# Last output block and final norm in two token halves of 128, the other output blocks of layer 1 with both activation parts in one 512-column product

## The chip, the cores and the metric

The kernel runs on one core of one Trainium2 chip. The metric is device time in microseconds of one execution. Three runs of the kernel before gave a median of 1247.78 us (1247.63 to 1248.28).

## What is computed

Two layers of a mixer on 256 latent tokens and 256 context tokens of width 2048, then a norm of the latent tokens. Each layer normalises and modulates its input, projects it by `w_in`, runs three branches (convolution, linear recurrence, windowed attention), gates each, and ends in one output projection. Cut to what the change touches:

```python
    x = x + gate * (jnp.concatenate([y_conv, y_lru, y_attn], axis=-1) @ w_out)
    ...
def rmsnorm(x, g):
    xf = x.astype(jnp.float32)
    y = xf * lax.rsqrt(jnp.mean(xf * xf, axis=-1, keepdims=True) + EPS)
    return (y * g.astype(jnp.float32)).astype(x.dtype)
    ...
    return rmsnorm(x, final_g)
```

In the last layer only the 256 latent tokens (`LAT`) go through the output projection.

## The kernel before, in words

Everything is held transposed: the 128 partitions are features, the free axis is tokens, and a tensor of 2048 features is 16 tiles (`DT`) of 128 x `TOK` (512: first 256 latent, then 256 context). A product with a 2048 x 128 weight block is 16 k tiles, accumulated in one bank of PSUM. To keep accuracy in the reduced format float32r, weights and activations are split in a high part (rounded) and a low part (the rest), and each k tile takes three products: high weights x high activations (line 826), high weights x low activations (L827), low weights x high activations (L828). Every product loads its own 128 x 128 weights.

Each layer has 56 blocks of 128 output features in the order of `BLOCKS`; the last 16 (`B_OUT` to `NB - 1`) are the output projection. The weight stream is one list (`stream()`): SyncE loads a block of 1 MB into one of three raw slots; ScalarE rounds half a block into `w_hi` (`hi`, L1050), VectorE subtracts to get `w_lo` (`lo`, L1410), into one of four slots each. Both run two blocks ahead of TensorE, in the program order of the loops over `gb`. Every engine has its own program; they meet only in semaphores (`C.up` raises, `C.at` names a value to wait for).

Of layer 1's output projection (its activations lie in the token columns 256 to 511 of `h_hi` and `h_lo`, `y_parts`):

- TensorE, `mm_half` (L803): half a block of eight k tiles, twice a block; waits for `lo` and for the bank (two banks in turn, `released`). It raises `mm`.
- VectorE, `evac` (L1581): once a block is done, Y = PSUM x gate + Y for the 256 latent tokens (L1614). In VectorE's order it stands behind both `lo` halves of the block two ahead. Then `rms_add` (L1467) adds a squared tile to the running sum.
- ScalarE, `square` (L1066, the operation is L1079) squares the new tile of Y and `scaled` (L1083) writes the tile times `final_g` to the other half of Y's columns.
- After the last block: TensorE sums over partitions with a product by ones (`rms_mm`, L714: the sum of 15 squares at L723, then the last square at L725), ScalarE takes the root (`rms_std`, L1101), VectorE the reciprocal (`rstd`, L1549) and five multiplications over 2, 4, 4, 4 and 2 tiles (`FINAL`, L1890), and SyncE stores each of the five pieces when it is ready (L618).

Layer 0's last two blocks are already done in token halves of 256 (`evac_lat`, `rms_mm_half` with L731 and L733), with their waits hidden by other products.

Of the kernel before, what the change touches and what calls it, by code (L numbers as in the profile page):

```python
# [24 lines left out]
P = 128  # L25
# [42 lines left out]
SPAN = (1, 1, 1, 1, 1, 1, 1, 1)  # L68
GROUPS = len(SPAN)
XPART = 2  # L70
FINAL = (2, 4, 4, 4, 2)
HALF = DT // 2 * P
BRIDGE = [14, 4, 6, 8]
SPLIT_FROM = NB - 2
# [177 lines left out]
def program(nc, io, known):  # L252
    ctx = ExitStack()
    with ctx:
# [12 lines left out]
        NRAW = 3  # L267
        GLU_SLOT, Q_SLOTS, KV_SLOT, BD_SLOT = NRAW, (NRAW + 1, NRAW + 2), NRAW + 3, NRAW + 4
        ADA0_SLOTS, CHUNK_SLOTS = (*range(NRAW), GLU_SLOT, KV_SLOT, BD_SLOT), Q_SLOTS
        hh = sb("h_hi", [P, DT, TOK], F32R)  # L270
        hl = sb("h_lo", [P, DT, TOK], F32R)
        Y = sb("Y", [P, DT, TOK])
        raw = sb("raw", [P, NRAW, DT * P])
        wh = sb("w_hi", [P, 4, DT // 2 * P], F32R)
# [166 lines left out]
        def done_before(l, b):  # L441

            last = PLAN.get(b - 1, []) if l == 0 else PLAN[NB] if b == OPEN[l] else []
            return [a[:2] for a in last if a[2] == DT - 1]

        def width(l, b):
            return TOK if l == 0 or BLOCKS[l][b][0] in BOTH else LAT

# [14 lines left out]
        def in_halves(gb):  # L463
            return SPLIT_FROM <= gb < NB

        def final_parts():
            return [(sum(FINAL[:i]), n) for i, n in enumerate(FINAL)]

        def squares(l):

            return (2, 3) if l else (0, 1, 2, 3)
# [45 lines left out]
        def _(sp):  # L517
# [49 lines left out]
            for i, item in enumerate(STREAM):  # L567
# [45 lines left out]
                    residual(item[1] - B_OUT - 2)  # L613
                elif item[0] == "open" and item[1] < 2:
                    residual(DT - 2 + item[1])
            for m, n in final_parts():
                sp.wait_ge(*C.at("final", m))
                sp.dma_start(io["out"][:, m:m + n, :], Y[:, m:m + n, 0:LAT]).then_inc(*C.up("stored", by=16))  # L618
            sp.wait_ge(*C.ago("stored"))


# [23 lines left out]
        def _(pe):  # L645
# [67 lines left out]

            def rms_mm(l):  # L714

                n = TOK if l < LAYERS else LAT
                if l == 0:
                    pe.wait_ge(*C.at("rms_add", l, DT - 1))
                    mm(psS[:, 0, 0:n], ones, T[:, 4, 0:n], start=True, stop=True).then_inc(*C.up("rms_mm", l))
                    return  # L720
                assert l == LAYERS
                pe.wait_ge(*C.at("rms_add", l, DT - 2))
                mm(psS[:, 0, 0:n], ones, T[:, 4, 0:n], start=True, stop=False)  # L723
                pe.wait_ge(*C.at("rms_sq", l, DT - 1))
                mm(psS[:, 0, 0:n], ones, T[:, squares(l)[(DT - 1) % 2], 0:n], start=False, stop=True).then_inc(*C.up("rms_mm", l))  # L725

            def rms_mm_half(s):

# [74 lines left out]
            def mm_half(gb, j, s=None):  # L803
                l, b = divmod(gb, NB)
                n = width(l, b)
                ps = bank(gb)
                u = unit(l, b, j)
                pe.wait_ge(*C.at("lo", u))
                if j == 0 and b == PW_AT + 1:
                    pe.wait_ge(*C.at("pw_out", l, CT - 2))  # L810
                elif j == 0 and b >= OPEN[l] and s != 1:
                    pe.wait_ge(*released(gb - 2 if b - 2 >= OPEN[l] else l * NB + b % 2))
                slot = u % 4
                t = y_parts(l) if b >= B_OUT else slice(0, n)
                cols = slice(0, n)
                if s is not None:
                    t = cols = tokens(s)
                if s == 1 and j == 0:
                    pe.wait_ge(*C.at("evac_lat", gb))
                for i in range(DT // 2):  # L820
                    at = j * DT // 2 + i
                    k = k_tile(b, at)
                    if b == B_OUT:
                        pe.wait_ge(*C.at("y_lo", l, k))
                    hi, lo = wh[:, slot, i * P:(i + 1) * P], wl[:, slot, i * P:(i + 1) * P]
                    mm(ps[:, cols], hi, hh[:, k, t], start=(at == 0), stop=False)  # L826
# [150 lines left out]
            for gb in range(GLOB):  # L977
# [14 lines left out]
                if in_halves(gb):  # L992
                    mm_half(gb, 0, 0)
                    mm_half(gb, 1, 0)
                    if b == NB - 1:
                        mm_half(gb - 1, 0, 1)
                        rms_mm_half(0)
                        mm_half(gb - 1, 1, 1)
                        mm_half(gb, 0, 1)
                        mm_half(gb, 1, 1)  # L1000
                    continue
                mm_half(gb, 0)

                for a in done_before(l, b):
# [29 lines left out]
                elif l == 0:  # L1034
                    for a in PLAN.get(b, []):
                        ada_mm(*a)
            rms_mm(LAYERS)


        @block.scalar  # L1040
        def _(act):
# [41 lines left out]
            def scaled(m):  # L1083
                fn(Y[:, m, LAT:TOK], Y[:, m, 0:LAT], ACT.Copy, scale=at["final_g"][:, m:m + 1]).then_inc(*C.up("scaled", m))

            def square_half(m, s):
# [9 lines left out]
                fn(tbuf[:, w], psS[:, 2 + s, w], ACT.Sqrt, scale=1.0 / D, bias=eps[:, 0:1]).then_inc(*C.up("rms_std", 1, s))  # L1096

            def rms_std(l):
                n = TOK if l < LAYERS else LAT
                act.wait_ge(*C.at("rms_mm", l))  # L1100
                fn(tbuf[:, 0:n], psS[:, 0, 0:n], ACT.Sqrt, scale=1.0 / D, bias=eps[:, 0:1]).then_inc(*C.up("rms_std", l))  # L1101

# [282 lines left out]
                    y_hi(l, b)  # L1385
            act.wait_ge(*C.at("derived"))
            fn(tiny[:, 0, 0:1], eps[:, 0:1], ACT.Sqrt).then_inc(*C.up("root_ahead"))
            square(LAYERS, DT - 1)
            rms_std(LAYERS)
            scaled(DT - 1)  # L1390


        @block.vector
        def _(dve):
# [149 lines left out]
                h_list([(QT, 1)] + [(k, i) for k in range(QT + 1, 2 * QT) for i in range(2)])  # L1544

            def rstd(l):
                n = TOK if l < LAYERS else LAT
                dve.wait_ge(*C.at("rms_std", l))
                V.reciprocal(tbuf[:, 0:n], tbuf[:, 0:n]).then_inc(*C.up("rstd", l))  # L1549
                dve.wait_ge(*C.ago("rstd"))  # L1550

            def h_chunk(c):

# [27 lines left out]
            def evac(gb):  # L1581
# [200 lines left out]
            for gb in range(GLOB):  # L1782
# [48 lines left out]
                    lo(unit(0, gb + 2, 1))  # L1831
                if gb == GLOB - 1:
                    rms_add(LAYERS, DT - 2)
                if in_halves(gb):
                    evac_half(gb, 0)
                elif l or b != B_OUT - 1:
                    evac(gb)
# [56 lines left out]

# [69 lines left out]
```

## Time and profile before

| what | before |
|---|---|
| median of three runs | 1247.78 us |
| the profiled execution | 1247.64 us |
| its span, first to last record | 1245.7 us |
| TensorE busy | 1203.5 us, 97% |
| VectorE busy | 827.3 us, 66% |
| ScalarE busy | 555.5 us, 45% |
| mean granted TensorE clock | 0.995 of full |
| DMA moved | 236.34 MB, 190 GB/s |

How to read it: times in all rows are from the span's start. A busy record of TensorE (PE) has a modelled end and overlaps the next one, so the spacing of starts, not the length of a record, tells what a product costs; PEld are the weight loads, which run beside the products. DVE is VectorE, ACT ScalarE, SPq the queue of SyncE that issues DMAs.

### The profile page before, as it was taken

Reading aid. Unit: us, or ns where it says so; the run is one execution under the profiler, and the core shown is the slowest. Engines: PE = TensorE matmul, PEld = TensorE weight load, DVE = VectorE, ACT = ScalarE, POOL = GpSimd, SP = SyncE. Lnnn points to the kernel's source line nnn. Section 1 sums busy time; section 2 is a strip of 40 time slices with the busy share of each in tenths; the row PEclk is TensorE's granted clock in tenths of the full one; section 3 lists DMA queues with packets and bytes.
Section 4 is the critical chain, followed back from the end, with each engine's and each line's share of the span. In section 5 each row is a group of like instructions: output and inputs, shape, how many; then the busy total and the mean of one; then the engine's idle time right before and its main releaser. Section 6 shows DMA issues by size and latency. Waiting matters only on the chain.

```text
span 1245.7 us, 16857 instructions
## 1 busy us (share of the span) xinstructions
PE 1203.5 (97%) x6790; PEld 971.9 (78%) x6790; DVE 827.3 (66%) x1268; ACT 555.5 (45%) x873; POOL 10.2 (1%) x13
## 2 busy tenths in 40 slices
PE   2899999999999999999999999999999999999996
PEld 1556777667778777886888887988978988899995
DVE  5444546767666677663787877695899977647554
ACT  5222446652224433464342222354865445475542
POOL 0000100000000000000000001000000000000000
PEclk9999999999999999999999999999999999999998
DMA  9999856556753354211549776343332634325542
GB/s 334 350 349 348 251 208 240 203 207 248 270 218 127 140 187 185 75 68 68 177 158 344 259 286 229 109 145 134 138 106 77 223 133 149 132 102 199 177 170 68
DMA packets 80893, 236.34 MB, mean 190 GB/s; under 512 B 9392, under 2 KB 54192, under 8 KB 59440
## 3 DMA queue, kind: packets, MB, share of 16 engines
q1 hardware_dynamic: 80816, 235.27, 53.5%
q8 instruction: 53, 0.87, 0.3%
q14 instruction: 24, 0.20, 0.1%
HBM read 230.54 MB, written 2.10 MB: 187 GB/s over the span
## 4 chain that ended last, share of the span: by engine, by line
PE 84%; DVE 5%; SPq 4%; DMA 4%; ACT 2%; issue 1%; DVEq 0%; ACTq 0%
PE psum_block L826 21%; PE psum_block L828 21%; PE psum_block L827 21%; SPq L602 3%; PE psum_ada L656 3%; DMA raw<-in_w_ada 2%; PE psum_scores L908 1%; PE psum_scores L895 1%; DVE w_lo L1410 1%; PE psum_scores L928 1%; DVE Y L1691 1%; PE psum_ada L703 1%; DMA glu<-in_w_ada 1%; DMA bd<-in_w_ada 1%; PE psum_misc L955 1%; PE psum_scores L858 1%
## 5 line engine op out<-in xcount | busy, mean ns | idle before, releaser
L826 PE MATMUL psum_block<-h_hi,w_hi 128*128 128x256 f32 (+1 forms) x1648 | 562.4, 341 | 0.6 <-DVE h_lo L1402 0.3
L828 PE MATMUL psum_block<-h_hi,w_lo 128*128 128x256 f32 (+1 forms) x1648 | 553.3, 336 | 0.0
L827 PE MATMUL psum_block<-h_lo,w_hi 128*128 128x256 f32 (+1 forms) x1648 | 553.2, 336 | 0.0
L1410 DVE TENSOR_TENSOR w_lo<-raw,w_hi 128x1024 fp32r<-128x1024 f32 x210 | 254.7, 1223 | 287.7 <-ACT w_hi L1050 287.4
L1050 ACT ACTIVATE w_hi<-raw 128x1024 fp32r<-128x1024 f32 x210 | 220.2, 1057 | 419.5 <-PE psum_block L828 380.0
L826 PEld LDWEIGHTS psum_block<-h_hi,w_hi 128*128 128x128 f32 x1648 | 312.7, 190 | 53.4 <-issue 17.6
L827 PEld LDWEIGHTS psum_block<-h_lo,w_hi 128*128 128x128 f32 x1648 | 312.9, 190 | 33.6 <-issue 2.6
L828 PEld LDWEIGHTS psum_block<-h_hi,w_lo 128*128 128x128 f32 x1648 | 312.7, 190 | 32.4
L1691 DVE SCALAR_TENSOR_TENSOR Y<-glu,small,Y 128x512 f32<-128x512 f32 (+1 forms) x240 | 130.4, 612 | 0.0
L1217 ACT ACTIVATE T<-psum_scores,stats 128x512 f32<-128x512 f32 (+1 forms) x48 | 28.9, 615 | 46.5 <-DVE stats L1739 46.5
L1104 ACT ACTIVATE h_hi<-T,ada 128x256 fp32r<-128x256 f32 x64 | 28.5, 501 | 41.6 <-DVE T L1486 41.6
L1410 DVE TENSOR_TENSOR w_lo<-qreg,w_hi 128x1024 fp32r<-128x1024 f32 (+1 forms) x16 | 17.5, 1092 | 33.4 <-ACT w_hi L1050 32.3
L656 PE MATMUL psum_ada<-raw,cstat 128*32 128x512 f32 x320 | 38.5, 598 | 1.1 <-DVE ada L1475 1.1
L1444 DVE SCALAR_TENSOR_TENSOR kv<-raw,cstat,kv 128x2048 f32<-128x2048 f32 x15 | 35.2, 2344 | 1.1 <-DMA raw<-in_w_ada 1.0
L1223 ACT ACTIVATE T<-T,stats 128x512 f32<-128x512 f32 (+1 forms) x48 | 27.4, 640 | 13.6 <-DVE stats L1749 13.6
L1648 DVE SCALAR_TENSOR_TENSOR Y<-qreg,small,Y 128x512 f32<-128x512 f32 x48 | 32.5, 746 | 0.0
L1050 ACT ACTIVATE w_hi<-qreg 128x1024 fp32r<-128x1024 f32 (+1 forms) x16 | 15.1, 945 | 33.8 <-DMA qreg<-in_w_blocks 33.8
L1079 ACT ACTIVATE T<-Y 128x512 f32<-128x512 f32 (+1 forms) x46 | 24.4, 544 | 10.8 <-DVE Y L1614 8.6
L1492 DVE SCALAR_TENSOR_TENSOR h_lo<-T,ada,h_hi 128x256 fp32r<-128x256 f32 x64 | 27.8, 480 | 1.3 <-ACT h_hi L1104 1.3
L1486 DVE SCALAR_TENSOR_TENSOR T<-Y,A,tbuf 128x256 f32<-128x256 f32 x64 | 27.6, 481 | 0.6
L1456 DVE SCALAR_TENSOR_TENSOR qreg<-glu,cstat,qreg 128x2048 f32<-128x2048 f32 x12 | 27.6, 2345 | 0.0
L1467 DVE TENSOR_TENSOR T<-T 128x512 f32<-128x512 f32 (+1 forms) x42 | 25.1, 598 | 2.8 <-ACT T L1079 1.3
(222 smaller groups left out, 1215.0 us busy)
## 6 DMA issues: line engine op xcount, KB each, us to landing
raw<-in_w_blocks SPq DMA_DIRECT2D x105, 1024.0 KB, 4.8
raw<-in_w_ada SPq DMA_DIRECT2D x75, 1024.0 KB, 7.1
glu<-in_w_ada SPq DMA_DIRECT2D x11, 1024.0 KB, 8.1
qreg<-in_w_blocks SPq DMA_DIRECT2D x8, 896.0 KB, 11.6
kv<-in_w_ada SPq DMA_DIRECT2D x5, 1024.0 KB, 12.0
bd<-in_w_ada SPq DMA_DIRECT2D x5, 1024.0 KB, 11.9
Y<-in_xT SPq DMA_DIRECT2D x8, 512.0 KB, 8.0
T<-in_xT SPq DMA_DIRECT2D x16, 256.0 KB, 5.8
```

The costliest lines, as they stand in the source:

```text
L602: sp.dma_start(dst, src).then_inc(C.sem(f"raw{SLOT[i]}"), 16)
L656: last = mm(psA[32 * j:32 * j + 32, :], cstat[:, c_at(k):c_at(k) + 32], w[:, j * TOK:(j + 1) * TOK], start=(k == 0), stop=(k == DT - 1), t ...
L826: mm(ps[:, cols], hi, hh[:, k, t], start=(at == 0), stop=False)
L827: mm(ps[:, cols], hi, hl[:, k, t], start=False, stop=False)
L828: last = mm(ps[:, cols], lo, hh[:, k, t], start=False, stop=(at == DT - 1))
L1050: fn(wh[:, u % 4, 0:cols.stop - cols.start], raw_of(item)[:, cols], ACT.Copy).then_inc(*C.up("hi", u))
L1104: fn(hh[:, k, tokens(i)], T[:, k % 2, tokens(i)], ACT.Identity, bias=ada[:, l, i, SHIFT * DT + k:SHIFT * DT + k + 1]).then_inc(*C.up("h_hi ...
L1217: fn(T[:, g, k0:TOK], psS[:, g, k0:TOK], ACT.Exp, scale=SCALE, bias=st[:, 1, g:g + 1], accum_out=st[:, 2, g:g + 1]).then_inc(*C.up("att_ex ...
L1410: V.tensor_tensor(wl[:, u % 4, 0:n], raw_of(item)[:, cols], wh[:, u % 4, 0:n].bitcast(F32), ALU.subtract).then_inc(*C.up("lo", u))
L1444: stt(acc, w, cstat[:, c_at(k):c_at(k) + 1], acc, ALU.mult, ALU.add).then_inc(*C.up("gate_acc", k))
L1648: stt(out, x, lcw[:, c, k:k + 1], out, ALU.mult, ALU.add).then_inc(*C.up("taps", l, t, d))
L1691: stt(out, x, dwh[:, c:c + 1], out, ALU.mult, ALU.add).then_inc(*C.up("conv", l, t, k))
```

## The change

It does two things, both in layer 1's output projection.

One: the high and low activations become two halves of one tensor, `parts`. In the output blocks of layer 1 except the last (`apart`), the products of lines 826 and 827 become one with 512 columns: its first 256 columns of PSUM hold high x high, to which low weights x high activations are added, its other 256 high weights x low activations. `evac` adds the second half of the bank to Y first (a new operation, with a wait behind it), then the first half as before.

Two: the last block runs in two halves of 128 tokens (`LAST`): products of the first token half for both halves of k, then those of the second; evacuation, square, sum, root, reciprocal, multiplications and store are done for each token half. The multiplications go over 8 and 8 tiles for the first half, 6, 6 and 4 for the second.

```diff
-FINAL = (2, 4, 4, 4, 2)
+FINAL = ((8, 8), (6, 6, 4))
+LAST = LAT // len(FINAL)
...
-        hh = sb("h_hi", [P, DT, TOK], F32R)
-        hl = sb("h_lo", [P, DT, TOK], F32R)
+        parts = sb("h_parts", [P, 2, DT, TOK], F32R)
+        hh, hl = parts[:, 0, :, :], parts[:, 1, :, :]
...
+        def apart(l, b):
+
+            return l == 1 and B_OUT <= b < NB - 1
...
-            for m, n in final_parts():
-                sp.wait_ge(*C.at("final", m))
-                sp.dma_start(io["out"][:, m:m + n, :], Y[:, m:m + n, 0:LAT]).then_inc(*C.up("stored", by=16))
+            for s in range(len(FINAL)):
+                for m, n in final_parts(s):
+                    sp.wait_ge(*C.at("final", s, m))
+                    sp.dma_start(io["out"][:, m:m + n, last_tokens(s)], Y[:, m:m + n, last_tokens(s)]
+                                 ).then_inc(*C.up("stored", by=16))
...
+            def last_rms_mm(s):
+
+                w = last_tokens(s)
+                pe.wait_ge(*C.at("rms_add", LAYERS, DT - 2))
+                mm(psS[:, s, w], ones, T[:, 4, w], start=True, stop=False)
+                pe.wait_ge(*C.at("rms_sq", LAYERS, DT - 1, s))
+                mm(psS[:, s, w], ones, T[:, squares(LAYERS)[(DT - 1) % 2], w], start=False, stop=True
+                   ).then_inc(*C.up("rms_mm", LAYERS, s))
+
+            def last_block_half(j, s):
+
+                gb = GLOB - 1
+                u = unit(1, NB - 1, j)
+                if s == 0:
+                    pe.wait_ge(*C.at("lo", u))
+                    if j == 0:
+                        pe.wait_ge(*released(gb - 2))
+                elif j == 0:
+                    pe.wait_ge(*C.at("evac_lat", gb))
+                w = last_tokens(s)
+                t = slice(LAT + w.start, LAT + w.stop)
+                ps = bank(gb)[:, w]
+                for i in range(DT // 2):
+                    at = j * DT // 2 + i
+                    k = k_tile(NB - 1, at)
+                    hi, lo = wh[:, u % 4, i * P:(i + 1) * P], wl[:, u % 4, i * P:(i + 1) * P]
+                    mm(ps, hi, hh[:, k, t], start=(at == 0), stop=False)
+                    mm(ps, hi, hl[:, k, t], start=False, stop=False)
+                    last = mm(ps, lo, hh[:, k, t], start=False, stop=(at == DT - 1))
+                if j:
+                    last.then_inc(*C.up("mm_last", s))
...
+                    if apart(l, b):
+                        mm(segs(ps), hi, parts[:, :, k, t], start=(at == 0), stop=(at == DT - 1))
+                        last = mm(ps[:, cols], lo, hh[:, k, t], start=False, stop=(at == DT - 1), skip_group_check=True)
+                        continue
...
+                if gb == GLOB - 1:
+                    last_block_half(0, 0)
+                    last_block_half(1, 0)
+                    last_block_half(0, 1)
+                    last_rms_mm(0)
+                    last_block_half(1, 1)
+                    last_rms_mm(1)
+                    continue
...
-            square(LAYERS, DT - 1)
-            rms_std(LAYERS)
-            scaled(DT - 1)
+            last_square(0)
+            last_std(0)
+            last_scaled(0)
+            last_square(1)
+            last_std(1)
+            last_scaled(1)
...
+                    if apart(l, b):
+                        stt(Y[:, i, 0:LAT], bank(gb)[:, LAT:TOK], ada[:, l, 0, GATE * DT + i:GATE * DT + i + 1],
+                            Y[:, i, 0:LAT], ALU.mult, ALU.add).then_inc(*C.up("low_part", gb))
+                        dve.wait_ge(*C.ago("low_part"))
...
-            rstd(LAYERS)
-            dve.wait_ge(*C.ago("evac_dve"))
-            for m, n in final_parts():
-                for k in range(m, m + n):
-                    dve.wait_ge(*C.at("scaled", k))
-                V.tensor_tensor(Y[:, m:m + n, 0:LAT], Y[:, m:m + n, LAT:TOK],
-                                tbuf[:, 0:LAT].unsqueeze(1).to_broadcast([P, n, LAT]), ALU.mult).then_inc(*C.up("final", m))
+            last_evac(0)
+            last_rstd(0)
+            last_evac(1)
+            finals(0)
+            last_rstd(1)
+            finals(1)
```

`last_square`, `last_std`, `last_scaled`, `last_evac`, `last_rstd` and `finals` are the operations of before on the columns of one token half; `last_evac(0)` raises `evac_lat`.

## Rows read from the trace of the kernel before

**Rows 1.** The page: busy time by engine (sections 1 and 4).
```profile
PE 1203.5 (97%) x6790; PEld 971.9 (78%) x6790; DVE 827.3 (66%) x1268; ACT 555.5 (45%) x873; POOL 10.2 (1%) x13
...
PE 84%; DVE 5%; SPq 4%; DMA 4%; ACT 2%; issue 1%; DVEq 0%; ACTq 0%
```

**Rows 2.** Timeline (start, length, engine, line, operation): first product of two blocks.
```profile
1140.20 0.28 PE L826 MATMUL psum_block<-h_hi,w_hi 128*128 128x256 f32 x1
...
1226.61 0.28 PE L826 MATMUL psum_block<-h_hi,w_hi 128*128 128x256 f32 x1
```

**Rows 3.** Stretch of the last block: busy by engine, granted clock, DMA share, GB/s.
```profile
1226.61:1232.37 5.76, 5.76 (x51) 5.76 (x50) 1.24 (x3) 2.31 (x4) 0.00 (x0) 1.00 0.00 0
```

**Rows 4.** Timeline of the tail.
```profile
1232.37 0.59 PE L723 MATMUL psum_scores<-T,small 128*128 128x256 f32 x2
1232.57 0.48 DVE L1614 SCALAR_TENSOR_TENSOR Y<-psum_block,ada,Y 128x256 f32<-128x256 f32 x1 [4.37 <-PE psum_block L828]
1233.09 0.42 ACT L1079 ACTIVATE T<-Y 128x256 f32<-128x256 f32 x1 [3.42 <-DVE Y L1614]
...
1234.29 0.47 ACT L1101 ACTIVATE tbuf<-psum_scores,eps 128x256 f32<-128x256 f32 x1 [0.79 <-PE psum_scores L725]
...
1234.80 1.75 DVE L1549 RECIPROCAL tbuf<-tbuf 128x256 f32<-128x256 f32 x1 [1.75 <-ACT tbuf L1101]
1236.59 4.70 DVE L1890 TENSOR_TENSOR Y<-Y,tbuf 128x512 f32<-128x512 f32 x5
1237.31 4.67 SPq L618 DMA_DIRECT2D out<-Y  x5
```

**Rows 5.** DMA of 1236 to 1246 us, GB/s in forty slices of 0.25 us.
```profile
GB/s 0 0 0 0 0 0 0 0 25 319 348 324 33 152 356 344 340 291 381 340 344 340 348 295 381 332 336 348 311 377 340 340 356 340 303 45 0 0 0 0
```

**Rows 6.** Timeline of TensorE, layer 0: 512-column products, the first and the twelfth.
```profile
599.66 0.39 PE L826 MATMUL psum_block<-h_hi,w_hi 128*128 128x512 f32 x1
...
602.15 0.39 PE L828 MATMUL psum_block<-h_hi,w_lo 128*128 128x512 f32 x1
```

**Rows 7.** Groups by line: count, busy us, mean ns, idle before.
```profile
L858 PE MATMUL psum_scores<-Y,bd 128*128 128x512 f32 x32 | 14.4, 592 | 0.0
L928 PE MATMUL psum_scores<-T,kv 128*128 128x512 f32 x32 | 14.4, 592 | 0.0
```

**Rows 8.** Timeline of VectorE: low activation parts, and a block's evacuation.
```profile
1143.50 1.42 DVE L1402 TENSOR_TENSOR h_lo<-Y,h_hi 128x256 fp32r<-128x256 f32 x4
...
1223.34 0.48 DVE L1614 SCALAR_TENSOR_TENSOR Y<-psum_block,ada,Y 128x256 f32<-128x256 f32 x1
```

**Rows 9.** Timeline of products and weight loads around one 128-column product, layer 0.
```profile
369.10 0.22 PE L886 MATMUL psum_scores<-rounded 128*128 128x128 f32 x1
...
369.44 0.40 PE L882 MATMUL psum_scores<-kv_r,T_r 128*128 128x512 f32 x1
...
369.10 0.19 PEld L881 LDWEIGHTS psum_scores<-bd_r,T_r 128*128 128x128 f32 x1
369.21 0.19 PEld L882 LDWEIGHTS psum_scores<-kv_r,T_r 128*128 128x128 f32 x1
```

**Rows 10.** Timeline: eight transposes of 128 columns.
```profile
602.38 1.03 PE L908 MATMUL psum_scores<-rounded,T 128*128 128x128 f32 x8
```

**Rows 11.** Groups by line: one operation at other sizes.
```profile
L1549 DVE RECIPROCAL tbuf<-tbuf 128x512 f32<-128x512 f32 x1 | 3.4, 3353 | 4.3 <-ACT tbuf L1101 4.3
...
L1890 DVE TENSOR_TENSOR Y<-Y,tbuf 128x1024 f32<-128x1024 f32 x3 | 3.5, 1219 | 0.0
...
L1890 DVE TENSOR_TENSOR Y<-Y,tbuf 128x512 f32<-128x512 f32 x2 | 1.4, 688 | 0.0
```

**Rows 12.** Timeline of TensorE: layer 0's norm product inside the stream.
```profile
796.38 0.59 PE L731 MATMUL psum_scores<-T,small 128*128 128x256 f32 x2
...
797.36 0.28 PE L827 MATMUL psum_block<-h_lo,w_hi 128*128 128x256 f32 x1
```

**Rows 13.** Stretch of one microsecond, all engines, clock, DMA share, GB/s.
```profile
656.00:657.00 1.00, 1.00 (x6) 0.81 (x6) 0.89 (x1) 0.35 (x1) 0.00 (x0) 1.00 1.33 245
```

More of the change, by code:

```diff
@@ L464, in in_halves, with final_parts, last_tokens @@
             return SPLIT_FROM <= gb < NB
-        def final_parts():
-            return [(sum(FINAL[:i]), n) for i, n in enumerate(FINAL)]
+        def final_parts(s):
+            return [(sum(FINAL[s][:i]), n) for i, n in enumerate(FINAL[s])]
+        def last_tokens(s):
+            return slice(s * LAST, (s + 1) * LAST)
         def squares(l):
@@ L714, in rms_mm @@
             def rms_mm(l):
[L716 to L725, printed above, removed]
+                assert l == 0
+                pe.wait_ge(*C.at("rms_add", l, DT - 1))
+                mm(psS[:, 0, :], ones, T[:, 4, :], start=True, stop=True).then_inc(*C.up("rms_mm", l))
+            def last_rms_mm(s):
[26 more added lines that the diff above has]
+                    last.then_inc(*C.up("mm_last", s))
             def rms_mm_half(s):
@@ L1036, in _ @@
                         ada_mm(*a)
-            rms_mm(LAYERS)
         @block.scalar
@@ L1084, in scaled, with last_square, last_std, last_scaled @@
                 fn(Y[:, m, LAT:TOK], Y[:, m, 0:LAT], ACT.Copy, scale=at["final_g"][:, m:m + 1]).then_inc(*C.up("scaled", m))
+            def last_square(s):
+                w = last_tokens(s)
+                act.wait_ge(*(C.at("evac_dve", GLOB - 1) if s else C.at("evac_lat", GLOB - 1)))
+                act.wait_ge(*C.at("rms_add", LAYERS, DT - 3))
+                fn(T[:, squares(LAYERS)[(DT - 1) % 2], w], Y[:, DT - 1, w], ACT.Square).then_inc(*C.up("rms_sq", LAYERS, DT - 1, s))
+            def last_std(s):
+                w = last_tokens(s)
+                act.wait_ge(*C.at("rms_mm", LAYERS, s))
+                fn(tbuf[:, w], psS[:, s, w], ACT.Sqrt, scale=1.0 / D, bias=eps[:, 0:1]).then_inc(*C.up("rms_std", LAYERS, s))
+            def last_scaled(s):
+                w = last_tokens(s)
+                fn(Y[:, DT - 1, LAT + w.start:LAT + w.stop], Y[:, DT - 1, w], ACT.Copy, scale=at["final_g"][:, DT - 1:DT]
+                   ).then_inc(*C.up("last_scaled", s))
             def square_half(m, s):
@@ L1098, in rms_std @@
             def rms_std(l):
-                n = TOK if l < LAYERS else LAT
+                n = TOK
                 act.wait_ge(*C.at("rms_mm", l))
@@ L1546, in rstd, with last_evac, last_rstd, finals @@
             def rstd(l):
-                n = TOK if l < LAYERS else LAT
                 dve.wait_ge(*C.at("rms_std", l))
-                V.reciprocal(tbuf[:, 0:n], tbuf[:, 0:n]).then_inc(*C.up("rstd", l))
+                V.reciprocal(tbuf[:, :], tbuf[:, :]).then_inc(*C.up("rstd", l))
                 dve.wait_ge(*C.ago("rstd"))
+            def last_evac(s):
+                w = last_tokens(s)
+                dve.wait_ge(*C.at("mm_last", s))
+                stt(Y[:, DT - 1, w], bank(GLOB - 1)[:, w], ada[:, 1, 0, GATE * DT + DT - 1:GATE * DT + DT], Y[:, DT - 1, w],
+                    ALU.mult, ALU.add).then_inc(*(C.up("evac_dve", GLOB - 1) if s else C.up("evac_lat", GLOB - 1)))
+            def last_rstd(s):
+                w = last_tokens(s)
+                dve.wait_ge(*C.at("rms_std", LAYERS, s))
+                V.reciprocal(tbuf[:, w], tbuf[:, w]).then_inc(*C.up("rstd", LAYERS, s))
+                dve.wait_ge(*C.ago("rstd"))
+            def finals(s):
+                w = last_tokens(s)
+                for m, n in final_parts(s):
+                    for k in range(m, min(m + n, DT - 1)):
+                        dve.wait_ge(*C.at("scaled", k))
+                    if m + n == DT:
+                        dve.wait_ge(*C.at("last_scaled", s))
+                    V.tensor_tensor(Y[:, m:m + n, w], Y[:, m:m + n, LAT + w.start:LAT + w.stop],
+                                    tbuf[:, w].unsqueeze(1).to_broadcast([P, n, LAST]), ALU.mult).then_inc(*C.up("final", s, m))
             def h_chunk(c):
@@ L1833, in _ @@
                     rms_add(LAYERS, DT - 2)
+                    continue
                 if in_halves(gb):
```

## The prediction

> **What bounds the kernel now.** I read the page first: TensorE is busy 97% of the span and holds 84% of the chain that ended last [rows 1]. Then the timeline of TensorE in the last hundred microseconds. From the first output block of layer 1 to the last one (1140.20 to 1226.61) it runs 15 blocks of 48 products of 256 columns without a gap: 86.41 us / 720 = 0.120 us a product, 5.76 us a block [rows 2]. The granted clock of the last block is full speed, 2.4 GHz, and no DMA is under way in it [rows 3]. So each nanosecond taken off a product there reaches the end. After the last product (1232.37) comes a serial tail of 13.3 us [rows 4]: evacuation, square, sum over partitions, root, reciprocal, five multiplications, and the store. The DMA view of the last ten microseconds shows what ends last [rows 5]: 2.10 MB leave at about 340 GB/s, nearly without a pause from 1239.5 to 1244.8, though the last piece is computed at 1241.29. The end of the kernel is the store's rate, counted from when its first pieces are ready.
>
> **Part 1, both activation parts in one product (15 blocks).** Per k tile, two products of 256 columns become one of 512. In layer 0 eleven spacings of 512-column products take 602.15 - 599.66 = 2.49 us, 0.226 each [rows 6]. Two of 256 cost 0.240. The gain is 0.0133 us per k tile (0.2267 and 0.120 lie on a line of 0.0133 + 0.000417 per column), x 16 x 15 = 3.2 us. The product now reads two segments far apart. The nearest rows are layer 1's gate products, which read two segments, against the attention products, which read 512 columns in one run: 592 ns both [rows 7]. Those segments lie one tile apart instead of sixteen; I take no cost, and 3.2 us (all of the gain gone) as the other end. A gain beyond 0.0133 is excluded, since the columns streamed are the same.
>
> The evacuation of each of these blocks becomes two dependent operations: one more of 0.48 us on VectorE. The evacuation of the fourteenth block now starts at 1223.34 [rows 8], 2.5 us after that block's last product (1226.61 - 5.76 = 1220.85), because `lo` of a later block stands before it; with the second one it ends some 3.5 us after. The bank is wanted again 5.55 us after that last product, so it costs nothing; it would with 2 us more on VectorE. In the first output block TensorE comes to its last four k tiles at 1140.20 + 12 x 0.347 = 1144.36 and then every 0.35 us; their low parts are made from 1143.50 on, 0.35 us each [rows 8]: ready about half a microsecond ahead. No cost, but little slack. The last block's weights are split two blocks ahead; that stays hidden. The last block so starts at 1226.61 - 3.2 = 1223.4.
>
> **Part 2, the last block in two token halves.** Its 48 products of 256 columns become 96 of 128. If the columns alone counted, the line above would give 0.067 us each. But each product loads its own 128 x 128 weights. One 128-column product of this number format stands between 512-column ones in the score groups of layer 0 [rows 9]: from its start (369.10) to that of the second product behind it (369.44) are 0.34 us, of which the 512-column one is 0.227, so it cost 0.11; and the two weight loads after it begin 0.11 apart (369.10, 369.21), the second only when the first is in the array. Eight 128-column transposes in a row take 1.03 us with the last one's drain, at most 0.129 each [rows 10]. I take 0.108 as the spacing. The Trainium skill, TensorE: Matmul & The Clock Gate, section LDWEIGHTS (loading the stationary operand), gives columns / 1.2 ns, 107 ns for 128 columns; by that rule, the trace agrees, and it speaks against splitting this block. So 96 x 0.108 = 10.37 us instead of 5.76.
>
> On top: the second token half waits for `evac_lat`, the evacuation of the first, with nothing of TensorE's own queued between; all later products stand behind that wait. Before, VectorE starts 0.20 us after the last product's slot and takes 0.48 [rows 4]; for 128 columns I put 0.17 + 0.345 (the 1.04 ns per element by which 1024 and 512 elements differ, 1219 and 688 ns [rows 11]), 0.04 for the signal and about 0.15 to load and restart: 0.7 us idle, 0.5 to 0.9. And the first half's norm product now stands between products: in layer 0 the same four passes at 256 columns delay the stream by 797.24 - 796.38 = 0.86 us [rows 12] (797.24 is 0.12 before the next start); at 128 columns four loads of 0.108 bound it below, 0.43, and I take 0.45.
>
> TensorE after: 1223.4 + 5.18 (first half) + 0.7 + 2.59 + 0.45 + 2.59 = 1234.9, against 1232.37: 2.6 us later in spite of part 1.
>
> **The tail.** Evacuation of the second half starts at 1235.1 and ends at 1235.45. By then the first half's root and reciprocal (3353 ns for 512 elements, 1755 for 256 [rows 4, 11], so 0.96 for 128) are done, about 1234.0: in the shadow of the last 24 products. The multiplications of the first half are queued on VectorE ahead of the second reciprocal: two of 1024 elements, 1.22 each, to 1237.8. Square, sum and root of the second half end about 1236.7 in their shadow. Then reciprocal 0.96 and multiplications 0.95 + 0.95 + 0.69, with handoffs: 1241.3. Before, the multiplications ended at 1236.59 + 4.70 = 1241.29. So VectorE's end does not move: half-size reciprocal and earlier multiplications give back what TensorE lost.
>
> **The store.** The first piece (512 KB) is ready at 1235.45 + 1.22 = 1236.7. Before, the first was issued at 1237.31 and bytes moved from about 1238.1: 0.8 us. Now they move from 1237.5, and each next piece is ready before the one ahead has left, so 2.10 MB run through without a pause. But pieces of a row are 512 bytes, not 1 KB. The nearest rows: 1 KB pieces move at about 340 GB/s [rows 5], and in a microsecond in which the gate weights come in, in pieces of 64 numbers (256 bytes), the engines move 245 [rows 13]. I take the middle, 290: 7.24 us, so the last byte at 1244.7, against 1244.8. At 340 it would be 1.1 us earlier, at 245 1.3 later. The Trainium skill, DMA: Bandwidth & Descriptors, Specifications, asks for at least 512 B for line rate; by it alone the sum would be 1.1 us lower. No row here has 512-byte pieces.
>
> **Sum.** -0.1 us on the profiled execution (1247.64 with a span of 1245.7, 1.9 around it): 1247.5. That run lay 0.14 under the median of the three, 1247.78, so 1247.7. Bounds of this case: below, -1.1 (store), -0.2 (shorter restart) and -0.5 (the small operations at 128 columns start from fewer fixed costs than the line says): 1245.9. Above, a spacing of 0.120 as now, where the 0.0133 comes on top of the load (+1.15), +1.3 (store), +0.2: 1250.3.
>
> **Rivals.** (a) *The columns set the pace of the halves*: 0.067 instead of 0.108, if consecutive loads overlap further in a long run than after one product. TensorE ends 96 x 0.041 = 3.9 us earlier, and all after it shifts: 1243.7, faster. The records of the loads, 0.19 long at spacings of 0.12, overlap already and speak for it; the two loads 0.11 apart [rows 9] and the transposes against. The skill's TensorE page, section Back-to-back issue gap, has 81 ns for sustained 128-column products; worked out, 96 x 0.027 = 2.6 us earlier, 1245.1. Chance 7%.
> (b) *The merged product gains nothing*: a two-segment read or the switch between a 512- and a 256-column product eats the 0.0133 us. It decides from the price where the pair costs 0.240 instead of 0.227. Then the last block starts 3.2 us later, nothing hides it, and the run takes 1250.9: slower. Only [rows 7] speak against, for another number format. 7%.
> (c) *The clock falls in the last block.* At 0.108 a product the array streams half of the time, and it idles 0.7 us once; the last block before has the full clock [rows 3] with the array nearly always streaming. If the level falls to 1.2 GHz over the second token half, its 48 products cost up to 5.2 us more: about 1252.9. 5%.
> (d) *The split does not do what it says*: the store's start is all that counts, and it moves only 0.6 us earlier; that is inside my forecast.
>
> **How the numbers follow.** Forecast case 80%, (a) 7, (b) 7, (c) 5, other 1. About 0.2% (2.5 us) is what a measurement of this kernel can tell from no change: 1245.3 to 1250.3. Faster: (a), 7%, plus 2% of the forecast's lower end. Slower: (b), (c), and 2% of its upper end, 14%. Same: 77%. The forecast's own bounds, 1245.9 to 1250.3, hold close to 8 in 10, and I keep them.
>
> **What would show it.** Products of the 14 undisturbed blocks: a start every 0.227 + 0.120 us, 5.55 us a block. Last block: starts 0.107 to 0.113 apart, one gap of about 0.7 us in the middle; its last product near 1235. VectorE's last multiplication near 1241.3. The store flowing from 1237.5 without a pause to about 1244.7, at 290 GB/s. Starts 0.067 apart would show (a), a block of 5.76 us (b), a granted clock under 1 before 1235 (c). A store at 340 GB/s would take a microsecond off and leave the verdict.

## The result

| | before | after |
|---|---|---|
| median | 1247.86 us (16 runs) | 1250.03 us (16 runs) |
| ratio, 95% interval | | 1.0018 [1.0012, 1.0024] |
| span of the profiled execution | 1245.7 us | 1248.0 us |
| TensorE instructions | 6790 | 6602 |

The change makes the kernel 0.18% slower. That is less than the 0.2% that I called the limit of what can be told, but the interval does not contain 1: my forecast was 0.1 us less, in effect no movement, and the 2.2 us more are real. The profile after, against the rows of before.

The page, against [rows 1]: 188 fewer products, yet TensorE is busy 4.6 us more.
```profile
PE 1208.1 (97%) x6602; PEld 965.0 (77%) x6602; DVE 834.8 (67%) x1285; ACT 557.2 (45%) x876; POOL 10.2 (1%) x13
```
The timeline of TensorE, against [rows 2] and [rows 6]: start, length, engine and line. L862 is the merged product, L863 the low weights' product.
```profile
1140.27 0.40 PE L862 MATMUL psum_block<-h_parts,w_hi 128*128 128x512 f32 x1
1140.50 0.28 PE L863 MATMUL psum_block<-h_parts,w_lo 128*128 128x256 f32 x1
1140.62 0.40 PE L862 MATMUL psum_block<-h_parts,w_hi 128*128 128x512 f32 x1
1140.86 0.28 PE L863 MATMUL psum_block<-h_parts,w_lo 128*128 128x256 f32 x1
1140.98 0.40 PE L862 MATMUL psum_block<-h_parts,w_hi 128*128 128x512 f32 x1
...
1225.07 0.22 PE L756 MATMUL psum_block<-h_parts,w_hi 128*128 128x128 f32 x1
```
240 pairs, each a merged product and a low weights' product, take 1225.07 - 1140.27 = 84.80 us, 0.3533 each: not the 0.360 of before, and not the 0.347 that I had summed. The next product starts 0.23 or 0.24 us after a 512-column one and 0.11 or 0.12 us after a 256-column one. Half of the gain of part 1 is missing, 1.6 us.

The last block, against [rows 2, 3]:
```profile
1225.24 0.27 PE L758 MATMUL psum_block<-h_parts,w_lo 128*128 128x128 f32 x1
...
1230.27 0.27 PE L758 MATMUL psum_block<-h_parts,w_lo 128*128 128x128 f32 x1
1230.98 0.33 PE L756 MATMUL psum_block<-h_parts,w_hi 128*128 128x128 f32 x1 [0.44 <-DVE Y L1622]
1231.15 0.27 PE L757 MATMUL psum_block<-h_parts,w_hi 128*128 128x128 f32 x1
...
1233.72 0.43 PE L734 MATMUL psum_scores<-T,small 128*128 128x128 f32 x2
...
1234.28 0.27 PE L757 MATMUL psum_block<-h_parts,w_hi 128*128 128x128 f32 x1
```
The stretch of this block (busy by engine, granted clock, DMA share, GB/s):
```profile
1225.07:1236.85 11.78, 11.34 (x103) 11.20 (x101) 3.03 (x6) 3.28 (x7) 0.00 (x0) 1.00 0.00 1
```
45 spacings of the first half take 1230.27 - 1225.24 = 5.03 us, 0.112 each. In the middle stands the wait for the evacuation of the first half: from 1230.27 to 1231.15 are 0.88 us where two spacings would be 0.22, so 0.66 idle. The norm product costs 1234.28 - 0.11 - 1233.72 = 0.45.

The tail, against [rows 4]:
```profile
1236.85 0.43 PE L734 MATMUL psum_scores<-T,small 128*128 128x128 f32 x2
1237.11 0.35 DVE L1622 SCALAR_TENSOR_TENSOR Y<-psum_block,ada,Y 128x128 f32<-128x128 f32 x1 [1.35 <-PE psum_block L758]
...
1237.51 2.36 DVE L1640 TENSOR_TENSOR Y<-Y,tbuf 128x1024 f32<-128x1024 f32 x2
...
1238.77 5.56 SPq L627 DMA_DIRECT2D out<-Y  x5
1239.79 0.95 DVE L1629 RECIPROCAL tbuf<-tbuf 128x128 f32<-128x128 f32 x1
1240.77 2.43 DVE L1640 TENSOR_TENSOR Y<-Y,tbuf 128x768 f32<-128x768 f32 x3
```
TensorE is done at 1236.85 instead of 1232.37. The first piece of the store is issued at 1238.77, 1.5 us later than before, and what comes out of it is the store's flow, 1238 to 1248 us in slices of 0.25 us, against [rows 5]:
```profile
GB/s 0 0 0 0 0 0 29 291 291 293 291 225 274 317 279 293 287 293 254 276 307 289 289 285 225 328 287 281 295 254 303 295 289 289 287 287 109 0 0 0
```
Bytes move from 1239.6 to 1247.1, without a pause, at about 290 GB/s between dips and 285 with them; before it was 340, dips included.

### The profile page after: what moved, and what is told of

Read it like the earlier page. It is cut to its first block, busy times and chain, and to the rows that moved or that the text cites. A ratio compares the mean times of both kernels' runs of the same rounds, so it can differ in the third digit from the quotient of the medians.

```text
span 1248.0 us, 16510 instructions
## 1 busy us (share of the span) xinstructions
PE 1208.1 (97%) x6602; PEld 965.0 (77%) x6602; DVE 834.8 (67%) x1285; ACT 557.2 (45%) x876; POOL 10.2 (1%) x13
## 4 chain that ended last, share of the span: by engine, by line
PE 82%; DVE 6%; SPq 4%; DMA 4%; ACT 3%; issue 1%; DVEq 0%; ACTq 0%
PE psum_block L865 18%; PE psum_block L866 18%; PE psum_block L867 18%; PE psum_block L862 5%; SPq L610 3%; PE psum_ada L666 3%; PE psum_block L863 2%; DMA raw<-in_w_ada 2%; DVE w_lo L1477 2%; DVE Y L1786 2%; PE psum_scores L934 1%; PE psum_scores L947 1%; DMA glu<-in_w_ada 1%; PE psum_ada L713 1%; DMA bd<-in_w_ada 1%; PE psum_misc L994 1%
## 5 line engine op out<-in xcount | busy, mean ns | idle before, releaser
L865 PE MATMUL psum_block<-h_parts,w_hi 128*128 128x512 f32 (+1 forms) x1392 | 490.0, 352 | 0.7 <-DVE h_parts L1469 0.3
L866 PE MATMUL psum_block<-h_parts,w_hi 128*128 128x512 f32 (+1 forms) x1392 | 480.8, 345 | 0.0
L867 PE MATMUL psum_block<-h_parts,w_lo 128*128 128x512 f32 (+1 forms) x1392 | 480.8, 345 | 0.0
L865 PEld LDWEIGHTS psum_block<-h_parts,w_hi 128*128 128x128 f32 x1392 | 263.6, 189 | 53.6 <-issue 17.6
L866 PEld LDWEIGHTS psum_block<-h_parts,w_hi 128*128 128x128 f32 x1392 | 263.8, 189 | 33.4 <-issue 2.6
L867 PEld LDWEIGHTS psum_block<-h_parts,w_lo 128*128 128x128 f32 x1392 | 263.6, 189 | 32.4
L862 PE MATMUL psum_block<-h_parts,w_hi 128*128 128x512 f32 x240 | 84.8, 399 | 0.0
L863 PE MATMUL psum_block<-h_parts,w_lo 128*128 128x256 f32 x240 | 67.4, 281 | 0.0
L862 PEld LDWEIGHTS psum_block<-h_parts,w_hi 128*128 128x128 f32 x240 | 45.1, 188 | 11.3
L1168 ACT ACTIVATE h_parts<-T,ada 128x256 fp32r<-128x256 f32 x64 | 28.6, 503 | 42.6 <-DVE T L1553 42.6
L863 PEld LDWEIGHTS psum_block<-h_parts,w_lo 128*128 128x128 f32 x240 | 45.3, 189 | 0.0
L1559 DVE SCALAR_TENSOR_TENSOR h_parts<-T,ada,h_parts 128x256 fp32r<-128x256 f32 x64 | 27.8, 481 | 1.3 <-ACT h_parts L1168 1.3
```

The lines of the kernel that those rows point to most:

```text
L862: mm(segs(ps), hi, parts[:, :, k, t], start=(at == 0), stop=(at == DT - 1))
```

## Experiments

Profiled executions differ by up to 1.5 us in when the output blocks of layer 1 begin (1139.6 to 1141.0 us), also between kernels that are the same up to there. Where I compare profiles I therefore count from the first product of these blocks to the end of the span: 105.5 us before, 107.7 after.

**The two parts apart.** The kernel before with part 1 alone, so without the change to the last block (shown is TensorE's edit; the joined tensor and the second evacuation operation go with it):
```diff
+                    if apart(l, b):
+                        mm(segs(ps), hi, parts[:, :, k, t], start=(at == 0), stop=(at == DT - 1))
+                        last = mm(ps[:, cols], lo, hh[:, k, t], start=False, stop=(at == DT - 1), skip_group_check=True)
+                        continue
```


> Part 1 of the change alone: the merged products in the first 15 output blocks of layer 1, last block, norm and store as before. By the trace of the changed kernel the pair of products takes 0.353 us instead of 0.360, so 15 blocks save 1.6 us, all of which must reach the end: 1246.2 us, ratio 0.9987. If the changed kernel's slower pair comes from something that the merged product does to the stream only together with the split last block, the gain would be the 3.2 us that I had summed: 1244.6. If merging also disturbs the tail (a later evacuation ahead of the last block), nothing is gained: 1247.8.

Measured: 1245.71 us, ratio 0.9986 [0.9977, 0.9994]. From the first output block to the end 103.9 us, 1.6 less than before. The other way round, the last block in halves and no merged product:
```diff
-            return l == 1 and B_OUT <= b < NB - 1
+            return False
```


> Part 2 alone: last block, norm and store in two token halves, all other blocks as before. If the parts add, this is the changed kernel plus 1.6 us: 1251.6 us, ratio 1.0030. By the prediction's own terms for this part (products 0.108 apart, store at 290 GB/s) it would be 1250.7. If the split were innocent and the merge the cause of the loss, it would lie at or under 1247.8.

Measured: 1251.56 us, ratio 1.0033 [1.0021, 1.0046]; 109.3 us from the first output block, 3.8 more than before. The parts add up: -1.6 + 3.8 = 2.2 in the profiles, and in the medians, each against the kernel before in the same round, -1.8 + 4.0 = 2.2. Part 1 is a gain, and part 2 costs more than twice as much.

**Why the pair takes 0.353 us.** Three kernels, each the merge alone with one thing changed. Each ran once, so I read its profile and not its time. The merged product reads one run of 512 columns (the output blocks of layer 1 then compute something else):
```diff
-                        mm(segs(ps), hi, parts[:, :, k, t], start=(at == 0), stop=(at == DT - 1))
+                        mm(ps, hi, hh[:, k, :], start=(at == 0), stop=(at == DT - 1))
```


> As the merge alone, but the merged product reads 512 columns in one run of the high activations (latent and context columns) instead of two segments 16 tiles apart; this changes what is computed in the output blocks of layer 1, and only the spacing of the products counts. If the two-segment read costs the missing 6.7 ns of a pair, pairs are 0.347 us apart. If it is the change between a 512- and a 256-column product, or the 256-column product adding to columns just written, they stay at 0.353.

Measured: still 0.353, in the same pattern of 0.24 and 0.12 (1180.83 - 1179.77 = 1.06 us for three pairs). The timeline of TensorE in this kernel:
```profile
1179.77 0.40 PE L831 MATMUL psum_block<-h_parts,w_hi 128*128 128x512 f32 x1
1180.01 0.28 PE L832 MATMUL psum_block<-h_parts,w_lo 128*128 128x256 f32 x1
1180.13 0.40 PE L831 MATMUL psum_block<-h_parts,w_hi 128*128 128x512 f32 x1
1180.37 0.28 PE L832 MATMUL psum_block<-h_parts,w_lo 128*128 128x256 f32 x1
1180.48 0.40 PE L831 MATMUL psum_block<-h_parts,w_hi 128*128 128x512 f32 x1
1180.71 0.28 PE L832 MATMUL psum_block<-h_parts,w_lo 128*128 128x256 f32 x1
1180.83 0.40 PE L831 MATMUL psum_block<-h_parts,w_hi 128*128 128x512 f32 x1
```
So the two segments are not the cause. The work of other engines beside the stream is hardly the cause either: by the start times of the merge alone in nanoseconds, its 479 spacings repeat 233, 117, 241, 120, 236, 113 to within a nanosecond through all 15 blocks, whatever VectorE and ScalarE do at the time. The low product added to the other half of the bank:
```diff
-                        last = mm(ps[:, cols], lo, hh[:, k, t], start=False, stop=(at == DT - 1), skip_group_check=True)
+                        last = mm(ps[:, LAT:TOK], lo, hh[:, k, t], start=False, stop=(at == DT - 1), skip_group_check=True)
```


> As the merge alone, but the low weights' product is added to the second half of the bank instead of the first; the result is the same, since both halves are added up. If the loss comes from adding to columns that were written a given time before, the spacing of 0.353 us a pair changes (in the first half 512 columns lie between a column's two writes, in the second only 256). If it comes from the read or from the change of sizes, it stays at 0.353.

Measured: 0.353 again (103.9 us from the first output block, as in the merge alone). Which columns of PSUM are added to does not matter. Two merged products, then the two low ones:
```diff
-                        last = mm(ps[:, cols], lo, hh[:, k, t], start=False, stop=(at == DT - 1), skip_group_check=True)
+                        if i % 2:
+                            for o in (1, 0):
+                                last = mm(ps[:, cols], wl[:, slot, (i - o) * P:(i - o + 1) * P], hh[:, k_tile(b, at - o), t], start=False,
+                                          stop=(at == DT - 1 and o == 0), skip_group_check=True)
```


> As the merge alone, but two merged products are followed by the two low products, so that the size changes half as often. If each change of size costs, the mean of a pair falls from 0.353 to 0.350 us. If each two-segment read costs, it stays at 0.353. If a weight load is what is late behind a 256-column product, two of these in a row make it worse, above 0.353.

Measured: 0.348 a k tile, and 102.6 us from the first output block, 1.2 less than the merge alone. Its timeline, where consecutive products of one line are one row:
```profile
1180.24 0.62 PE L831 MATMUL psum_block<-h_parts,w_hi 128*128 128x512 f32 x2
1180.70 0.40 PE L834 MATMUL psum_block<-h_parts,w_lo 128*128 128x256 f32 x2
1180.93 0.63 PE L831 MATMUL psum_block<-h_parts,w_hi 128*128 128x512 f32 x2
```
Four products take 1180.93 - 1180.24 = 0.69 us (0.697 over the whole stream), where two alternating pairs take 0.707. The order of the sizes makes the difference. Is it each change of size? The same with groups of eight:
```diff
-                        if i % 2:
-                            for o in (1, 0):
+                        if i % 8 == 7:
+                            for o in range(7, -1, -1):
```


> As the merge alone, but eight merged products are followed by the eight low products of the half block. The mean of a k tile was 0.3533 us with alternating sizes and 0.3483 in groups of two. If the change of size is all that is lost, groups of eight come to the 0.2267 + 0.1200 = 0.3467 us that I had predicted, or a little above: 15 blocks then save 3.2 us against the kernel before: 1244.4 us, ratio 0.9974. If instead two short products behind two long ones are served faster than in a long run (in groups of two they stood 0.114 apart), eight are no better than two: 0.348 or more.

Measured: 1245.31 us, ratio 0.9983 [0.9974, 0.9992]. The timeline shows two things.
```profile
1140.44 2.00 PE L831 MATMUL psum_block<-h_parts,w_hi 128*128 128x512 f32 x8
1142.28 1.11 PE L834 MATMUL psum_block<-h_parts,w_lo 128*128 128x256 f32 x8
1143.23 2.47 PE L831 MATMUL psum_block<-h_parts,w_hi 128*128 128x512 f32 x8
1145.55 1.11 PE L834 MATMUL psum_block<-h_parts,w_lo 128*128 128x256 f32 x8
1146.49 2.00 PE L831 MATMUL psum_block<-h_parts,w_hi 128*128 128x512 f32 x8
...
1180.01 2.00 PE L831 MATMUL psum_block<-h_parts,w_hi 128*128 128x512 f32 x8
1181.85 1.11 PE L834 MATMUL psum_block<-h_parts,w_lo 128*128 128x256 f32 x8
1182.80 2.00 PE L831 MATMUL psum_block<-h_parts,w_hi 128*128 128x512 f32 x8
```
In the middle of the stream eight k tiles take 2.79 us, 0.349 each: above the 0.347 of my sum, and no better than groups of two. The eight long products take 1.84 (0.230 each, where the 0.2267 of [rows 6] would give 1.81), the short ones 0.95 (0.119). And in the first output block the second group takes 2.32 instead of 1.84: its last four tiles stand 0.5 to 0.9 us earlier than in the alternating order, and now TensorE waits for their low parts. VectorE makes these four parts in this row:
```profile
1143.73 1.43 DVE L1413 TENSOR_TENSOR h_parts<-Y,h_parts 128x256 fp32r<-128x256 f32 x4
```
That is about 0.35 us each, and the last four long products of the group are 0.33 to 0.34 apart. The slack that I had called little was half a microsecond, and this order used it up, 0.5 us in all.

So the loss stands behind a change of size, but not as a fixed price per change: that would have made eights the best. By the start times in nanoseconds, the spacings after the eight long products of a group are 233, 236, 228, 233, 231, 226, 227, 227, and those after the short ones 113, 119 and then 120: the first five long products behind the change are dearer by 28 ns together, the first short ones cheaper by 8, and only then does the stream come to the prices that it has with one size. In the alternating order the long products never do. What in the engine does it, these runs do not tell; it stays open.

**What 128-column products are bound by.** The changed kernel with 64 of the 128 columns of weights in the last block; its other 64 output features are left out:
```diff
-                    hi, lo = wh[:, u % 4, i * P:(i + 1) * P], wl[:, u % 4, i * P:(i + 1) * P]
-                    mm(ps, hi, hh[:, k, t], start=(at == 0), stop=False)
-                    mm(ps, hi, hl[:, k, t], start=False, stop=False)
-                    last = mm(ps, lo, hh[:, k, t], start=False, stop=(at == DT - 1))
+                    hi, lo = wh[:, u % 4, i * P:i * P + 64], wl[:, u % 4, i * P:i * P + 64]
+                    mm(ps[0:64, :], hi, hh[:, k, t], start=(at == 0), stop=False)
+                    mm(ps[0:64, :], hi, hl[:, k, t], start=False, stop=False)
+                    last = mm(ps[0:64, :], lo, hh[:, k, t], start=False, stop=(at == DT - 1))
```


> The changed kernel with only 64 of the 128 columns of weights loaded and used in the last block; the other 64 output features of that block are left out. If the weight load sets the spacing of 128-column products (0.112 us), half of it takes 0.054 and the columns take over: 0.067 us, and TensorE ends 96 x 0.045 = 4.3 us earlier. If something else of a product's overhead sets 0.112, the spacing does not move.

Measured, in one run: 0.060 us a product. Three loads and three products of it:
```profile
1229.13 0.14 PEld L756 LDWEIGHTS psum_block<-h_parts,w_hi 128*64 128x64 f32 x1
1229.19 0.14 PEld L757 LDWEIGHTS psum_block<-h_parts,w_hi 128*64 128x64 f32 x1
1229.25 0.14 PEld L758 LDWEIGHTS psum_block<-h_parts,w_lo 128*64 128x64 f32 x1
...
1229.67 0.22 PE L758 MATMUL psum_block<-h_parts,w_lo 128*64 128x128 f32 x1
1229.73 0.22 PE L756 MATMUL psum_block<-h_parts,w_hi 128*64 128x128 f32 x1
1229.79 0.22 PE L757 MATMUL psum_block<-h_parts,w_hi 128*64 128x128 f32 x1
```
Same columns streamed, same number of products, half the weights: 0.112 falls to 0.060, and the end moves 4.9 us ahead (102.8 us from the first output block). Fewer weights also mean fewer partitions of PSUM written, 64 for 128; but that cannot be what sets 0.112, since the 256-column products of before write twice as much each and stand only 0.120 apart. So the weight load sets the pace of the split block. The LDWEIGHTS section of the Trainium skill's TensorE: Matmul & The Clock Gate gives columns / 1.2 ns, from which 107 ns for 128 columns is an estimate; the run shows 112 in a long series.

**The wait in the middle.** The second token half goes to the other bank and waits for nothing of its own block:
```diff
-                    pe.wait_ge(*C.at("evac_lat", gb))
+                    pe.wait_ge(*released(gb - 1))
...
-                ps = bank(gb)[:, w]
+                ps = bank(gb - s)[:, w]
...
-                stt(Y[:, DT - 1, w], bank(GLOB - 1)[:, w], ada[:, 1, 0, GATE * DT + DT - 1:GATE * DT + DT], Y[:, DT - 1, w],
+                stt(Y[:, DT - 1, w], bank(GLOB - 1 - s)[:, w], ada[:, 1, 0, GATE * DT + DT - 1:GATE * DT + DT], Y[:, DT - 1, w],
```


> The changed kernel with the second token half of the last block accumulated in the other bank, which is free by then, so that its products need not wait for the evacuation of the first half. The gap of 0.66 us in the middle of TensorE's last block should go, and if that wait is on the path that sets the end, the whole 0.66 us: 1249.4 us. If VectorE's order (evacuation, reciprocal, evacuation, multiplications) takes the wait over, the time stays at 1250.0.

Measured: 1248.99 us, ratio 1.0013 [1.0004, 1.0022]. The last block shrinks from 11.78 us to 11.11:
```profile
1224.38:1235.49 11.11, 11.11 (x102) 11.11 (x101) 3.03 (x6) 3.27 (x7) 0.00 (x0) 1.00 0.01 1
```
The 0.66 us are the wait's, and the end moves by as much (107.0 us from the first output block against 107.7), so all of it was on the path. The ratios to the kernel before, 1.0018 and 1.0013, lie 0.6 us apart, though their intervals overlap.

**The store in rows of 512 bytes**, in the kernel before:
```diff
-                sp.dma_start(io["out"][:, m:m + n, :], Y[:, m:m + n, 0:LAT]).then_inc(*C.up("stored", by=16))
+                for h in range(2):
+                    w = slice(h * QB, (h + 1) * QB)
+                    sp.dma_start(io["out"][:, m:m + n, w], Y[:, m:m + n, w]).then_inc(*C.up("stored", by=16))
```


> The kernel before with each of its five pieces stored as two transfers of 128 tokens, so in rows of 512 bytes; nothing else changes. Bytes should move at 279 to 290 GB/s instead of 340. The pause after the first piece (0.5 us before) is filled by the slower transfer, so of 7.5 - 6.2 = 1.3 us about 0.8 to 1.3 should remain: 1248.7 to 1249.1. If the piece size were without effect, 1247.8; ten issues at 0.38 us each are 3.8 us, as long as the multiplications take, so the issues should not set the end.

Measured: 1248.81 us, ratio 1.0010 [1.0001, 1.0020]. DMA from 1236 to 1248 us, slices of 0.3 us:
```profile
GB/s 0 0 0 0 0 85 282 232 251 152 266 319 275 261 316 284 256 316 285 256 314 282 258 321 277 275 299 285 292 282 254 19 0 0 0 0 0 0 0 0
```
The rate falls from 340 to about 285 GB/s, and it costs 1.0 us in the profile (106.5 us from the first output block). This kernel also has ten transfers where there were five; but the changed kernel moves rows of 512 bytes in five transfers, at the same 285. So it is the shorter rows.

**What is left of the idea.** Merged products, last block in 256-column products as before, only the tail in token halves (pieces of 4, 6, 6 and 6, 6, 4 tiles; ScalarE squares and VectorE evacuates both halves before the first root and reciprocal). Cut to TensorE's part:
```diff
-                    last_block_half(0, 0)
-                    last_block_half(1, 0)
-                    last_block_half(0, 1)
+                    mm_half(gb, 0)
+                    mm_half(gb, 1)
                     last_rms_mm(0)
-                    last_block_half(1, 1)
                     last_rms_mm(1)
```


> Merged products in 15 blocks, the last block in 256-column products as before, and only what follows it (evacuation, square, sum, root, reciprocal, multiplications, store) in two token halves; pieces of 4, 6, 6 tiles for the first half and 6, 6, 4 for the second. If the loss of the changed kernel is the weight load of 128-column products, this keeps both gains: TensorE ends about 1230.8; first piece 3.5 us later, bytes from 1235.1, 7.5 us for 2.1 MB in 512-byte pieces, end of the span at 1243.5: 1245.4 us, ratio 0.998. If the token halves of the tail bring nothing by themselves, it equals the merge alone, 1246.2, or lies above it by the slower store.

Measured: 1245.39 us, ratio 0.9984 [0.9975, 0.9993]; 103.4 us from the first output block, 0.5 less than the merge alone. The medians of the two (1245.39 and 1245.71) are within each other's interval. With the merged products in groups of two on top:
```diff
-                        last = mm(ps[:, cols], lo, hh[:, k, t], start=False, stop=(at == DT - 1), skip_group_check=True)
+                        if i % 2 == 1:
+                            for o in range(1, -1, -1):
+                                last = mm(ps[:, cols], wl[:, slot, (i - o) * P:(i - o + 1) * P], hh[:, k_tile(b, at - o), t], start=False,
+                                          stop=(at == DT - 1 and o == 0), skip_group_check=True)
```


> Merged products in groups of two, the last block in 256-column products, the tail behind it in token halves. The groups of two save 240 x 0.0117 = 2.8 us against the kernel before, the halved tail 0.5: 1247.6 - 3.3 = 1244.3 us, ratio 0.9974. If the earlier end of TensorE runs into a wait of another engine (the evacuation of the fifteenth block), part of it is lost.

Measured: 1244.08 us, ratio 0.9971 [0.9959, 0.9982]: faster than both kernels. Its tail:
```profile
1229.83 0.38 PE L734 MATMUL psum_scores<-T,small 128*128 128x128 f32 x2
1230.03 0.61 DVE L1600 SCALAR_TENSOR_TENSOR Y<-psum_block,ada,Y 128x128 f32<-128x128 f32 x2 [3.85 <-PE psum_block L847]
...
1232.68 2.43 DVE L1618 TENSOR_TENSOR Y<-Y,tbuf 128x512 f32<-128x512 f32 x3
1233.40 5.58 SPq L627 DMA_DIRECT2D out<-Y  x6
```
The first piece is issued 3.6 us after TensorE's last product, against 4.9 before [rows 4]; the slower store takes most of that back, and 0.5 us remain against the groups of two without it (102.2 and 102.6 us from the first output block).

## Why the prediction was right or wrong

It said 1247.7 us and no change; measured were 1250.03 and 0.18% more. The time lies inside the stated range, near its upper end, and that is in part luck: the upper end was made of a spacing of 0.120 us in the last block and a store at 245 GB/s, and neither came. Step by step, on the profiled execution (a span of 1245.6 us forecast, 1248.0 found):

- **Part 1's gain: 3.2 us forecast, 1.6 found.** This is the step that failed, and two thirds of the miss. I took the price of each size from a stream of that size alone and added the two. In a stream that alternates, the pair costs 0.3533, not 0.3467; the part alone gained 1.6 us in its profile and 1.8 in its median. Rival (b), "the switch between a 512- and a 256-column product eats the 0.0133 us", had the place right and named its other end; half of it came true. The two-segment read, which I had weighed beside it, costs nothing here, as [rows 7] said.
- **The second evacuation operation: no cost forecast, none found.** For the fourteenth block the two stand at 1221.91 and 1222.43, and the last block, which takes its bank, starts at 1225.07.
- **The spacing in the split block: 0.108 forecast, 0.112 found** in the long series, 0.3 us over the block (11.78 us less the wait and the norm product, where the sum had 10.37). The mechanism was right and is shown by the halved weights. The 0.108 came from loads behind a single short product [rows 9]. Rival (a), columns setting the pace, is out as long as 128 columns of weights are loaded: neither its 0.067 nor its 0.081 came. With 64 columns of weights the 0.060 is near half of 0.112, and whether load or columns set it there is not shown.
- **The wait in the middle: 0.7 forecast, 0.66 found.** The norm product: 0.45 and 0.45. Both right.
- **VectorE's end.** I had it unmoved at 1241.3; it is 1243.20, later by the 1.9 us that TensorE is late. The order held, and the lengths nearly: reciprocal 0.95 for 0.96, multiplications 2.36 and 2.43 for 2.44 and 2.59, with the shadows as described. The evacuation starts 0.26 us after TensorE's slot instead of 0.2, and the first piece is issued 0.1 us later than TensorE alone explains.
- **The store: 7.24 us forecast, 7.5 found**, from 1239.6 instead of 1237.5, since TensorE is late. The rate between dips is the 290 GB/s that I took as the middle of 245 and 340, two rates of other transfers, so that it fits is luck; with the dips it is about 285, and 2.10 MB in 7.5 us are 280. The section Specifications of the Trainium skill's DMA: Bandwidth & Descriptors calls 512 B enough for line rate; here rows of 512 bytes move at 285 where 1 KB moves at 340, so the measurement decides against it. That the store runs through from its first piece and sets the end was right.
- **The clock** stayed at full speed through the last block (1.00 in its stretch): rival (c) is out.

Together 1.6 (the pairs) + 0.3 (the split block) + 0.1 (the output blocks start at 1140.27 instead of 1140.20) + 0.1 (to the first piece) + 0.3 (the store) = 2.4 us, the difference found. All of these point the same way. The forecast of no change was the difference of two sums of some 3 us, so misses of some tenths and one of half a term were enough to turn it.

## What to carry to other kernels

From 256 to 128 columns a product of this format with a full set of weights only went from 0.120 to 0.112 us: the weight load takes over, and splitting a block of such products by tokens doubles its loads. If a tail is to be pipelined, split what follows the products, not the products. And the cost of a mixed stream has to be read from a mixed stream: put equal sizes in small groups (two did best here), and check that the order does not reach an operand before it is made.

## What the hardware showed that I had not expected

- 240 pairs of a 512- and a 256-column product take 0.3533 us each, two and two 0.3483 per k tile, eight and eight 0.349; the streams of one size take 0.2267 and 0.120. Behind a change to 512 columns, five products pass before the spacing is back at 0.227.
- A 128-column product with 64 columns of weights takes 0.060 us, less than the 0.067 that a straight line through the 256- and 512-column streams gives. The part beside the columns is not the same 0.0133 at every size.
